# Causal attentions taken query block by query block, with token-major results, in a two-block fp32 transformer kernel

## The reference, cut to what matters

```python
h = _rmsnorm(x, attn_norm_g)
fq, fk, fv, sq, sk, sv, f_logit = split(h @ w_in)           # 8 fox heads and 8 sb heads of 64
c = cumsum(log_sigmoid(f_logit + b_forget))                 # one row per fox head
fox: logits = q.k/8 + c[t] - c[s] for s <= t;  p = softmax(logits);  o = p @ v
sb:  z = q.k/8;  A = sigmoid(z[t,s]) * prod_{s<j<t}(1 - sigmoid(z[t,j])) for s < t;  o = A @ v
mixed = concat(_rmsnorm(fox_o, fox_out_g), _rmsnorm(sb_o, sb_out_g))
x = x + mixed @ w_out
m = _rmsnorm(mem, mem_norm_g);  k, v = split(m @ w_mkv)     # the memory's keys and values
```

## Time and profile before

| | |
|---|---|
| time, median of 3 runs | 2115.2 us (2112.54 to 2116.13) |
| the profiled execution: its own time | 2112.78 us |
| its span in the trace | 2110.8 us |
| PE busy, share of the span | 2042.5 us, 97% |
| DVE, ACT, POOL busy | 1220.5, 757.8, 194.3 us |
| mean granted TensorE clock (1.0 is full speed) | 0.992 |

### The profile page before, as it was taken

One profiled execution on the slowest core, in us unless ns is written; L12 is line 12 of the kernel. 1 busy time (PEld: TensorE's weight loads), 2 busy tenths in 40 slices (PEclk: granted clock), 3 DMA queues, 4 the chain that ended last, 5 costly groups with the idle time before them and its releaser, 6 DMA issues.

```text
span 2110.8 us, 24369 instructions
## 1 busy us (share of the span) xinstructions
PE 2042.5 (97%) x10045; PEld 1689.7 (80%) x10045; DVE 1220.5 (58%) x1795; ACT 757.8 (36%) x1187; POOL 194.3 (9%) x96
## 2 busy tenths in 40 slices
PE   6999998999999999999989999999999999999998
PEld 5877876778888888899878788888877788888887
DVE  7565477847756656755557733333388776333333
ACT  4353253434433333532322432233352444232223
POOL 0000000000000000000000122222222012222221
PEclk9999999999999999999999999999999999999999
DMA  5212211211332223322312233223233013323331
GB/s 156 89 41 81 80 61 41 92 68 61 100 100 91 92 98 100 111 85 85 100 60 80 87 107 101 88 97 100 90 83 112 21 41 100 100 80 100 100 100 60
DMA packets 151374, 181.36 MB, mean 86 GB/s; under 512 B 14688, under 2 KB 120288, under 8 KB 151264
## 3 DMA queue, kind: packets, MB, share of 16 engines
q1 hardware_dynamic: 149632, 178.30, 26.2%
q10 hardware_dynamic: 1632, 1.51, 0.2%
HBM read 177.70 MB, written 2.10 MB: 85 GB/s over the span
## 4 chain that ended last, share of the span: by engine, by line
PE 87%; DVE 7%; ACT 2%; issue 2%; DMA 0%; DVEq 0%; ACTq 0%
PE bank L409 26%; PE bank L411 26%; PE bank L410 26%; PE bank L552 6%; PE bank L544 2%; DVE w_lo L843 1%; ACT w_hi L1544 1%; DVE rstd L893 1%; PE bank L707 1%; DVE arena L946 0%; PE bank L496 0%; DVE h_lo L859 0%; DVE arena L1453 0%; DMA raw<-w_in 0%; DVE arena L930 0%
## 5 line engine op out<-in xcount | busy, mean ns | idle before, releaser
L409 PE MATMUL bank<-h_hi,w_hi 128*128 128x512 f32 x1404 | 552.8, 394 | 10.0 <-issue 4.3
L411 PE MATMUL bank<-h_hi,w_lo 128*128 128x512 f32 x1404 | 547.5, 390 | 0.0
L410 PE MATMUL bank<-h_lo,w_hi 128*128 128x512 f32 x1404 | 547.4, 390 | 0.0
L1544 ACT ACTIVATE w_hi<-raw 128x1024 fp32r<-128x1024 f32 (+2 forms) x336 | 333.8, 1037 | 511.2 <-PE bank L411 509.0
L409 PE MATMUL bank<-g_hi,w_hi 128*128 128x512 f32 (+1 forms) x972 | 378.8, 390 | 10.5 <-DVE g_lo L857 4.3
L411 PE MATMUL bank<-g_hi,w_lo 128*128 128x512 f32 (+1 forms) x972 | 372.4, 383 | 0.0
L410 PE MATMUL bank<-g_lo,w_hi 128*128 128x512 f32 (+1 forms) x972 | 372.1, 383 | 0.0
L379 POOL TENSOR_TENSOR w_lo<-raw,w_hi 128x1024 fp32r<-128x1024 f32 (+1 forms) x78 | 191.5, 2456 | 1887.6 <-ACT w_hi L1544 1887.6
L901 DVE TENSOR_TENSOR resid<-bank,resid 128x512 f32<-128x512 f32 x304 | 206.5, 689 | 256.7 <-PE bank L411 256.0
L843 DVE TENSOR_TENSOR w_lo<-raw,w_hi 128x1024 fp32r<-128x1024 f32 (+1 forms) x258 | 305.7, 1210 | 78.7 <-ACT w_hi L1544 77.7
L409 PEld LDWEIGHTS bank<-h_hi,w_hi 128*128 128x128 f32 x1404 | 264.3, 188 | 69.5 <-issue 14.0
(11 more groups left out here) (186 smaller groups left out, 1786.4 us busy)
## 6 DMA issues: line engine op xcount, KB each, us to landing
raw<-w SPq DMA_DIRECT2D x64, 1024.0 KB, 5.2
raw<-w_up SPq DMA_DIRECT2D x22, 1024.0 KB, 5.0
raw<-a_w_in SPq DMA_DIRECT2D x16, 1024.0 KB, 5.3
raw<-w_in SPq DMA_DIRECT2D x12, 1024.0 KB, 5.4
raw<-w_down SPq DMA_DIRECT2D x11, 1024.0 KB, 5.0
raw<-w_mkv SPq DMA_DIRECT2D x8, 1024.0 KB, 5.4
raw<-a_w_out SPq DMA_DIRECT2D x8, 1024.0 KB, 5.0
raw<-w_out SPq DMA_DIRECT2D x4, 1024.0 KB, 5.4
```

The lines of the kernel that those rows point to most:

```text
L409: nc.tensor.matmul(dst, a_hi, b_hi, start=(k == 0), stop=False)
L410: nc.tensor.matmul(dst, a_hi, b_lo, start=False, stop=False)
L411: last = nc.tensor.matmul(dst, a_lo, b_hi, start=False, stop=(k == n - 1))
L1544: A(hi, src, ACT.Copy).then_inc(w_hi_done, 1)
```

## The change

It does these things:

- Both causal attentions go through `BLOCKS`: query block by query block, eight heads in each. A group of eight units fills one bank.
- `head_values` has the transposed probabilities (128 x 128) as the stationary operand and 64 value columns moving. The result is token-major: 128 tokens x 512 features in one bank.
- Fox probabilities are not normalised one by one. ACT's exp leaves the row sums in `row_sums`; when a group is done, DVE takes 8 reciprocals at once and multiplies the bank by them.
- -c[s] is a 65th row of the keys (`fox_k[64]`, filled by eight small DMAs that POOL issues) against a row of ones in `fox_q[64]`; `pick`, `neg_c` and the second score matmul go. POOL also does the memsets of `fox_q` for sb, after the last fox scores.
- The output norms work on rows: ACT squares with a sum, one Sqrt, one reciprocal, four multiplications by `mix_rs`. PE transposes the result (`turn_mixed`, 16 transposes for fox and 16 for sb), ACT makes the hi half and DVE the lo half from the bank with the gain. The matmuls with ones (`stat`) for both norms go.
- w_out comes as four quarters (4 row tiles x 512 columns), two for fox, two for sb. The first goes beside sb steps 31 to 34; the other three follow the attention. The other pieces beside the attentions move: mem_keys 2 per step in steps 0 to 7, 1 per step in 8 to 23, none in 24 to 31; mem_values in sb steps 2 to 17.
- `by_token` has 512 moving columns, in two chunks of four row tiles, and holds all four banks.

```diff
+    def tokens(name, block):
+        return [quarter(name, 0, block, tiles=1), quarter(name, 1, block, tiles=3)]
...
+        BLOCKS = [(h, i) for i in range(TT) for h in range(HEADS)]
+        FOX_FILL = [2] * 8 + [1] * 16 + [0] * 12
+        MIX_STEPS = range(31, 35)
-        FOX_PIECES, SB_PIECES = (4, 6, 13, 15, 21, 23, 29, 31), (4, 5, 8, 9, 12, 13, 17, 19, 31, 32)
+        FOX_PIECES, SB_PIECES = (5, 6, 9, 10, 18, 20, 26, 28), (1, 2, 7, 8, 11, 12, 16, 18, 21, 23)
...
+            pool.wait_ge(tile_full, KT)
+            G.memset(fox_q[HD:HD + 1, :, :], 1.0).then_inc(q_filled, 1)
+            pool.wait_ge(c_ready, 1)
+            for h in range(HEADS):
+                pool.dma_start(fox_k[HD:HD + 1, h, :], f_z[h:h + 1, :]).then_inc(c_loaded, 16)
...
+            def by_token(arrive=None, between=lambda: None):
+                first = tile.n
+                for half in range(2):
+                    wait_chunk()
+                    for t in range(TT):
+                        if half == 0:
+                            pe.wait_ge(tile_taken, first + t - 3)
+                        for k in range(4):
...
+                            nc.tensor.matmul(dst, a_hi, b_hi, start=(half == 0 and k == 0), stop=False)
+                            nc.tensor.matmul(dst, a_hi, b_lo, start=False, stop=False)
+                            last = nc.tensor.matmul(dst, a_lo, b_hi, start=False, stop=(half == 1 and k == 3))
...
             def fox_scores(h, i, dst):
-                return several([(dst, q, fox_k[:, h // 2, 0:n], True, False),
-                                (dst, pick[:, h:h + 1].to_broadcast([P, P]), neg_c[:, 0:n], False, True)])
+                return several([(dst, fox_q[0:HD + 1, h, P * i:P * i + P], fox_k[0:HD + 1, h, 0:P * (i + 1)], True, True)])
...
             def head_values(h, i, pt):
-                r = HD * (h % 2)
-                return several([(o_bank[r:r + HD, P * i:P * i + P], fox_v[:, k, HD * h:HD * h + HD],
-                                 pt[:, P * k:P * k + P], k == 0, k == i) for k in range(i + 1)])
+                return several([(o_bank[:, HD * h:HD * h + HD], pt[:, P * k:P * k + P],
+                                 fox_v[:, k, HD * h:HD * h + HD], k == 0, k == i) for k in range(i + 1)])
...
             finish_rstd(rstd[:, 0, :], rstd_col[:, 0:4])
-            for n in range(8):
-                r = slice(HD, P) if n % 2 == 0 else slice(0, HD)
-                V.memset(fox_q[r, n, :], 0.0)
...
+            split_low()
+            attention("fox", BLOCKS, causal, mixed_group("fox"), beside_fox)
+            normed()
...
             def beside_sb(s):
+                if 1 <= s < 3:
+                    take_mixed(h_hi, h_lo, "fox_out_g", 2 * s - 2)
+                    take_mixed(h_hi, h_lo, "fox_out_g", 2 * s - 1)
...
+            def beside_sb(s):
+                if s < 2:
+                    high_of_mixed(h_hi, "fox_out_g", 2 * s)
+                    high_of_mixed(h_hi, "fox_out_g", 2 * s + 1)
+                squares_of_group(4, SB_PIECES)(s)
```

More of the change, by code:

```diff
@@ L613, in _ @@
             by_token()
[L614 removed]
             pe.wait_ge(h_ready, h_n.n + KT)
             h_n.n += KT
[L617 to L624 removed]
+            pe.wait_ge(c_loaded, 16 * HEADS)
+            pe.wait_ge(q_filled, 1)
+            piece = Count()
@@ L625, in _, with beside_fox @@
+            def beside_fox(s):
+                for _ in range(FOX_FILL[s]):
+                    mem_keys(piece.n)
+                    piece.n += 1
+            attention("fox", BLOCKS, fox_scores, head_values, beside_fox, v_tiles=4)
+            for c in range(4):
                 by_feature()
             by_token()
-            by_token()
+            pe.wait_ge(q_filled, 3)
             def beside_sb(s):
-                if 3 <= s < 15:
-                    mem_values_of(s - 3)
-                elif s in BACK_STEPS:
-                    n = BACK_STEPS.index(s)
-                    back(n // KT, [n % KT], in_h=True)
@@ new lines, in beside_sb, with of_fox @@
+                if 2 <= s < 18:
+                    mem_values_of(s - 2)
+                if s in MIX_STEPS:
+                    of_fox(0, [s - MIX_STEPS[0]])
+            def of_fox(half, tiles):
+                if tiles[0] == 0:
+                    wait_chunk()
+                    pe.wait_ge(tile_taken, fox_end)
+                for n in tiles:
+                    dst = next_bank()
+                    full(split_sum(dst[:], w_tiles(4, slice(P * n, P * n + P), quarter_view), h_tiles(4)))
+                if tiles[-1] == 3:
+                    chunk.n += 1
@@ new lines, in _ @@
+            fox_end = tile.n + 4
+            attention("sb", BLOCKS, sb_scores, head_values, beside_sb, v_tiles=4)
+            of_fox(1, range(4))
+            pe.wait_ge(t_made, 3)
+            for n in range(4):
+                turn_mixed(n)
+            sb_end = tile.n
+            moving = [(g_hi[:, k, :], g_lo[:, k, :]) for k in range(4)]
+            wait_chunk()
+            first = tile.n
+            for k in range(4):
+                pe.wait_ge(tile_taken, sb_end - 3 + k)
+                for n in range(4):
+                    if k == 0:
+                        pe.wait_ge(tile_taken, first + n - 3)
+                    last = split_sum(tile_bank[(first + n) % 4][:], w_tiles(4, slice(P * n, P * n + P), quarter_view),
+                                     moving, part=range(k, k + 1))
+                    if k == 3:
+                        full(last)
@@ L647, in _ @@
+            chunk.n += 1
+            wait_chunk()
+            for n in range(4):
+                dst = next_bank()
+                full(split_sum(dst[:], w_tiles(4, slice(P * n, P * n + P), quarter_view), moving))
+            chunk.n += 1
             by_feature(arrive=h_n.n)
```

362 lines of the change are left out of this document (175 added, 187 removed).

## The result

The changed kernel takes 2102.98 us (median of 5 runs, 2100.47 to 2103.98), the kernel before 2114.47 (2112.54 to 2116.13) beside it: a ratio of 0.9948, 95% interval 0.9936 to 0.9960. It is faster by 11.5 us where 39.3 were forecast, and lies outside the range. The profiled execution has a span of 2100.7 us.

The account below looks back on a forecast made before the run. PE, busy 97%, was taken as the bound. Gains of 13.1 (fox), 13.6 (sb), 3.6 (start), 8.1 (token-major) and 0.9 sum to 39.3 us: 2073.5 from the profile, 2075.9 from the median, 2075 said; own range 2068 to 2082, wider 2062 to 2092.

Parts of the forecast that it names:

- Fox, order and waits: Fox attention: mem_keys stretches -0.5 us; idle 2.6 against 3.3 before, -0.7; fox falls from 84.4 to 71.3 us.
- one rival for sb: Chains bind in sb's long blocks, slower steps and one more clock dip: 2085 us, chance 0.20.
- Breaks and the values' turn: Each attention: full-width values end 32 tiling breaks, 8.0 us less; exchanging stationary and moving operands adds 0.6 us.
- breaks stay: Rival: the 65-row fox tile still breaks, +8 us, 2083; in both attentions +16, 2091; chance 0.12.
- stream only: Rival: value products cost only their 64-column stream, -9.2 us in fox, total 2063 us; chance 0.08.
- slower: Rival: value passes cannot hide their loads, 0.242 instead of 0.111 us each, +42 us, 2117; chance 0.04.
- second score matmul: Fox attention: removing this matmul from all eight heads saves 4.5 us, all on PE.
- sb with w_out: Second attention and output projection: sum of breaks, values, ones-matmul, transposes, idle and half clock, -13.6 us from 143.4.
- projections between the attentions: Token-major pair of chunks 1.35 us less, plus one ones-matmul removed, 0.9 us less.
- Start: Kernel start: memsets held DVE for 3.9 us; 3.6 us taken as gain, ends 2.4 and 5.
- third fox score: Start of fox attention: this score waits on splits, mask and exp, stalling PE 1.6 us.
- Token-major blocks: Projections and gates: 192 matmuls (23.1 us) become 96 (21.8 us) per pair of chunks; six pairs, -8.1 us.

Follow-up runs that it names:

- e11: Changed kernel with five fox split pieces moved one step later (10, 18, 20, 26, 28 to 11, 19, 21, 27, 29), nothing else: 2083.3 us.
- e2: Changed kernel with rows 65 to 127 of fox queries and keys zeroed and score matmuls over all 128 rows: 2091.37 us.
- e7: e4 with fox value products in the old form (V stationary in half the PE columns, 128 columns moving): 2086.11 us.
- e4: Changed kernel with mem_keys fill one per step over fox steps 3 to 34, split pieces moved, whole starting split put behind the attention: 2076.72 us.
- e8: e4 plus evacuation ahead of split piece and mask, with fox's turned blocks spread over sb steps 0, 1, 2, 6: 2075.42 us.
- e10: e4 plus evacuation ahead of split piece and mask, with memory values spread over sb steps 2 to 27 instead of 2 to 17: 2085.23 us.
- e1: Changed kernel with fox evacuation ahead of split piece and mask on VectorE, and five split pieces moved one step later: 2093.86 us.
- e9: Changed kernel with six unused 256-column split matmuls added to each of fox steps 24 to 34: 2091.3 us.
- e6: Changed kernel with evacuation first and fox scores over 128 rows with zeros, fill unchanged: 2088.48 us.
- e12: e4 with three of its eight split pieces put on the steps of the evacuations (10, 18, 26): 2082.31 us.
- e3: Changed kernel with fox value products in the old form (V stationary in half the PE columns, 128 columns moving): 2097.68 us.

## Why the prediction was wrong

**The step that failed is "Fox, order and waits".** It counted idle time at the start and the end only, 2.6 us, and it priced every step at full clock. DVE and ACT were called "both under PE's" from their sums per step; the row of VectorE at 123.34 shows that the order inside one step decides. The place was in the diff: FOX_PIECES has 10, 18, 26, and with 8 steps a block and values three steps late the evacuations fall on the same numbers. The timeline has 11.5 us of waits in the fox attention. The clock is the larger part: about 30 us at 0.50, of which PE would have needed half. 71.3, plus 8.9 more idle, leaves 13.8 of the 94.0: about half of 30, less the idle in it. The two are one failure: e11 moves five split pieces by one step and gives back 19.7 us, waits and clock together. Taken singly, the clock is worth 11.6 us with the waits left in place (e2).

**The clock should have been a rival for fox.** The prediction gave half clock a place at sb's start and in one rival for sb, always behind a wait. The long blocks of fox lost their only dense work by FOX_FILL's `[0] * 12`, which the prediction even counted ("512 keys 2.17 alone"). The kernel before had a piece of keys in each of these steps and a clock of 1.00.

**Held.** Breaks and the values' turn: the form alone 7.6 against 7.4 (e7); no break at 65 rows, since of the 1.81 us of a step at full clock 0.86 are scores, 0.61 three value products and 0.34 transposes, and the same step with 128 rows takes 1.81 in e2 (156.73 to 158.54). A value product is 0.20 to 0.21 (in e4 four in 160.19 - 158.49 - 0.86 = 0.84), where the two loads gave 0.22. The rivals "breaks stay" and "stream only" fall by that row, and "slower" with them. The second score matmul was not tested alone.

**Held as a sum.** sb with w_out 130.4 against 129.8, with 10.1 us idle for the 11 that were counted. At its start the wait is 3.48 us, and the clock falls behind it, as said. Its other terms were not measured one by one, and a second dip is there (0.83 from 320 to 330 us) where the sum kept only one, so it is in part luck that the sum came within 0.6 us. e8 shows that this start is not worth mending, e10 that the fill there was well placed. The projections between the attentions came down by 2.2 us in e4, where 1.35 + 0.9 was said.

**Nearly held.** Start: the first keys begin 2.9 us earlier instead of 3.6; VectorE still holds PE for 2.41 us there, behind a copy of memory columns. The third fox score waits 1.31 us, forecast 1.6. Token-major blocks: values 23.1 to 21.9, forecast 21.8, and the gates 4.7 less for 5.4.

**Missed beside it.** The projections behind fox took 67.7 where e4 has 65.3, 2.3 us of half clock carried over.

**Open.** What decides in steps that are neither dense nor idle. In the last 12 fox steps the changed kernel and e1 lost the clock, e2, e9 and e11 kept it in the profiled execution, e6 lost part of it. The runs of e6 and e11 scatter over 9 and 6 us, those of e4 over 1. A long wait often comes before a fall, but not always: 2.54 us brought none in e2, 0.97 us one in e1 and e6. With split matmuls beside the steps the clock was back in some 4 us (changed kernel at 126 us, e12 twice). Without them it stayed down over 20 us in the changed kernel and e1, but came back within 7 us in e3 and e6. So more rows, dense work and shorter waits all move this; not shown is a rule that would have told e1 from e11.

## What to carry to other kernels

Compare every table of steps with the steps in which a buffer is handed over: two short jobs on an engine that is 45% busy cost TensorE 1.1 to 3.1 us each time they met, and moving five entries of one table by one step was worth 19.7 us. When work is moved away from a stretch, price the stretch twice, at full and at half clock, if what is left there is narrow fp32 matmuls behind a wait. Some dense work beside each step was a second remedy of the same size; even useless work, some 8 us of it, left the kernel 11.7 us faster. A recipe that worked in one attention (spread the filler) cost 10.6 us in the next, whose pace another engine sets.

## What the runs showed of the hardware

- TensorE stood at the granted clock 0.50 (1.2 GHz) for 30 us while busy 93% of the time, with 65-row score matmuls, 64-column value products and transposes alone. It came back 4.4 us into the 512-column split matmuls that followed. The same stream of matmuls ran at 1.0 in e11, so the stream alone does not bring the clock down. The Trainium skill, TensorE: Matmul & The Clock Gate, Part 1: The HAM clock gate, says that activity releases the throttle; this stretch differs, since 28 us of busy records did not.
- Zeros in the other 63 rows of both operands, the same instructions otherwise, gave a clock of 1.0 (e2) and 11.6 us. With the same zeros it was at 0.50 from 178 to 184 us in e6.
- With 66 useless matmuls (e9) the clock was at 1.0, and 4.16 us a step became 2.85.
- A half-width stationary operand between full-width ones cost 0.31 us per step of 512 keys; 65 rows cost nothing against 128: 1.81 us a step in both.
- A value product with 64 moving columns takes 0.20 to 0.21 us, one with 128 takes 0.215: half the columns save next to nothing.
